# A two-layer decoder step on one core: a sixth set of expert weights, parameters as rows, inputs two pieces ahead

## What is computed

```python
def decoder_layer(x, pos, past_ckv, past_krope, h_pool, h_conv, h_sconv, mix_params, moe_params, ln_params):
    mix, st = token_mixer(x, pos, past_ckv, past_krope, h_pool, h_conv, h_sconv, *mix_params)
    x = layer_norm(ALPHA * x + mix, ln1_g, ln1_b)
    x = layer_norm(ALPHA * x + hier_moe(x, *moe_params), ln2_g, ln2_b)
    return x, st

# token_mixer: proj = x @ w_in; four branches (pooling, conformer convolution, latent
# attention, short convolution), each gated by a sigmoid; merged @ w_o
# hier_moe, 16 experts, the best 2 of one group of 4 for each token:
    h = silu(einsum('btd,edf->btef', x, w_gate)) * einsum('btd,edf->btef', x, w_up)
    h = h * comb[..., None]
    return einsum('btef,efd->btd', h, w_down)
```

## Time and profile before

| | us |
|---|---|
| median of 3 runs (lowest, highest) | 2022.55 (2022.48, 2024.47) |
| the profiled execution | 2009.65 |
| its span, first to last instruction | 2007.9 |

### The profile page before, as it was taken

One profiled execution on the slowest core, in us unless ns is written; L12 is line 12 of the kernel. 1 busy time (PEld: TensorE's weight loads), 2 busy tenths in 40 slices (PEclk: granted clock), 3 DMA queues, 4 the chain that ended last, 5 costly groups with the idle time before them and its releaser, 6 DMA issues. The chain is left out here.

```text
span 2007.9 us, 23969 instructions
## 1 busy us (share of the span) xinstructions
PE 1777.3 (89%) x9370; PEld 1205.9 (60%) x9370; DVE 799.0 (40%) x1603; ACT 445.8 (22%) x955; POOL 373.9 (19%) x398
## 2 busy tenths in 40 slices
PE   4998989999999997989569998889999999878990
PEld 3887666788888463333258776658888865533330
DVE  1596445433333350111426764554333315311116
ACT  0115534211111111111221254431111112111111
POOL 0003136000000001236100130530000004122545
PEclk6999899899999989989779988999999999889995
DMA  9203127222222647888470130443222344688984
GB/s 299 19 1 109 59 66 224 91 84 83 81 71 92 254 176 279 342 336 341 170 164 1 50 101 18 138 153 116 84 84 81 109 146 170 241 352 314 343 338 155
DMA packets 168728, 317.95 MB, mean 158 GB/s; under 512 B 63370, under 2 KB 125416, under 8 KB 150120
## 3 DMA queue, kind: packets, MB, share of 16 engines
q1 hardware_dynamic: 101144, 195.47, 27.6%
q0 software_dynamic: 37200, 116.84, 16.7%
q10 hardware_dynamic: 30272, 4.09, 1.5%
HBM read 355.74 MB, written 29.48 MB: 192 GB/s over the span
## 5 line engine op out<-in xcount | busy, mean ns | idle before, releaser
L1702 PE MATMUL ps<-space,xT 128*64 128x512 f32 x832 | 241.3, 620 | 29.5 <-DMA space<-in_exp_w_up 15.8
L1228 PE MATMUL ps<-space 128*128 128x272 f32 x1024 | 250.3, 392 | 0.0
L431 PE MATMUL ps<-xT,space 128*128 128x272 f32 (+1 forms) x960 | 225.3, 398 | 0.0
L1228 PEld LDWEIGHTS ps<-space 128*128 128x128 f32 x1024 | 194.6, 190 | 40.1
L431 PEld LDWEIGHTS ps<-xT,space 128*128 128x128 f32 (+1 forms) x960 | 184.0, 192 | 40.9
L1702 PEld LDWEIGHTS ps<-space,xT 128*64 128x64 f32 x832 | 73.5, 143 | 143.3 <-issue 140.1
L1236 PE MATMUL ps<-space 128*128 128x272 f32 x640 | 157.1, 392 | 0.0
L1959 DVE SCALAR_TENSOR_TENSOR space<-space,ps 128x256 f32<-128x256 f32 x32 | 21.5, 672 | 320.5 <-ACT space L1800 320.5
L1236 PEld LDWEIGHTS ps<-space 128*128 128x128 f32 x640 | 121.6, 190 | 25.1
L1228 PE MATMUL ps<-xT,space 128*128 128x272 f32 x512 | 128.5, 394 | 0.0
L1615 PE MATMUL ps<-space 128*128 128x512 f32 x256 | 115.7, 613 | 6.1 <-PEq L247 6.1
(11 more groups left out here) (376 smaller groups left out, 2428.5 us busy)
## 6 DMA issues: line engine op xcount, KB each, us to landing
space<-in_w_in SPq DMA_DIRECT2D x44, 1024.0 KB, 5.6
space<-in_exp_w_down SPq DMA_DIRECT2D x32, 1024.0 KB, 12.0
space<-in_exp_w_gate SPq DMA_DIRECT2D x24, 1024.0 KB, 13.1
space<-in_exp_w_up SPq DMA_DIRECT2D x24, 1024.0 KB, 14.9
space<-in_w_o SPq DMA_DIRECT2D x8, 1024.0 KB, 5.9
fifth<-in_exp_w_gate SPq DMA_DIRECT2D x8, 1024.0 KB, 17.1
fifth<-in_exp_w_up SPq DMA_DIRECT2D x8, 1024.0 KB, 19.3
space<-y_rows SPq DMA_DIRECT2D x16, 512.0 KB, 7.3
```

What stands on the lines that cost most here:

```text
L431: t = nc.tensor.matmul(ps[0:m, 2 * (n % 4) + h, 0:HN], w[:, f, c * P:c * P + m], k.xT[:, f, h, :], start=(f == 0), stop=(f == KD - 1))
L1228: t = m.matmul(out, w[:, f, :], x[:, f, :], start=(first and f == 0), stop=(f == H - 1), skip_group_check=True)
L1702: i = m.matmul(ps[r, 6 + t % 2, :], k.xgT[:, t % 2, f, r], gate_up_of(g)[:, f], start=(f == 0), stop=(f == KD - 1), skip_group_check=True)
```

## The change

It makes these edits.

1. The experts get a **sixth set** of weights, `k.sixth`, in place of the residual rows `k.x1` and of the end of `merged`. Its first load waits until the normed rows have landed in `x1_rows`; after its last use SP loads `x1` again from `x1_rows`, and DVE waits for that. All of ROUND, the loads and their semaphores follow. Tile 13 changes place with tile 9 in ORDER.
2. **Parameters are loaded as rows**: 14 DMAs put them into `prow` (43 rows) and `crow` (34 rows), PE transposes both at the head of `project` (three transposes), and ACT copies them to `k.par`. PE now waits for `s_prm`, ahead of all its work in the block. The DMAs are issued ahead of the constants by ACT in `load_start`, and by SP ahead of `first_inputs` in layer 0's `experts`. The copies into `x_rows` move from ACT in `load_start` to SP in `project`.
3. `first_inputs` issues only **two pieces** of `w_in`; the other five stand at the head of SP's queue in `project`.
4. The **landing of the stores** to `x_rows` is awaited by POOL at the head of layer 1's `project`.
5. Of the last two token tiles in layer 0, ACT turns features 0 to 3 and DVE features 4 to 7.

```diff
@@ load_start, ACT @@
             act.dma_start(k.ident[:], k.d["c_ident"]).then_inc(k.z_out, 16)
+            first_rows(k, act, 0)
...
-            for at, n, r in ROWS_OF:
-                act.dma_start(k.x_rows[at:at + r], k.d["x_prompt"][0, n:n + r, :]).then_inc(k.s_rows, 16)
...
+EARLY = 2
+def first_rows(k, queue, l):
+    d, one = k.d, bass.ds(l, 1)
+    for name, at, n in ROWS:
+        queue.dma_start(k.prow[at:at + n, :], d[name][one].rearrange("a (c p) -> (a c) p", p=P)).then_inc(k.s_prm, 16)
+    for at, lo, n, out in ((40, 0, P, 0), (41, P, QL - P, 0), (41, 0, 2 * P - QL, QL - P)):
+        queue.dma_start(k.prow[at:at + 1, out:out + n], d["q_norm_g"][one, lo:lo + n]).then_inc(k.s_prm, 16)
+    queue.dma_start(k.crow[0:CONVK, :], d["conv_w"][one].rearrange("a k n -> (a k) n")).then_inc(k.s_prm, 16)
+    queue.dma_start(k.crow[CONVK:CONVK + SCK, :], d["sconv_w"][one].rearrange("a k n -> (a k) n")).then_inc(k.s_prm, 16)
@@ first_inputs @@
-    for pos in range(SLOTS):
+    for pos in range(EARLY):
         projection(k, sp, l, pos)
@@ project: SP, ACT, POOL, PE @@
+            for pos in range(EARLY, SLOTS):
+                projection(k, sp, l, pos)
...
+            if l == 0:
+                for at, n, r in ROWS_OF:
+                    sp.dma_start(k.x_rows[at:at + r], d["x_prompt"][0, n:n + r, :]).then_inc(k.s_rows, 16)
...
-            (the 15 parameter DMAs on ACT's queue)
+            nc.scalar.copy(k.par[:, 0:43 + 2 * TAPS], ps[:, 0, 272:315 + 2 * TAPS])
...
+            if l:
+                pool.wait_ge(*due(k, n2.st, 16 * 5))
             pool.memset(k.up_p[:, :, 0:POOLH], 0.0).then_inc(k.a_zero, 1)
...
+            pe.wait_ge(*due(k, k.s_prm, 16 * 14))
+            nc.tensor.transpose(ps[:, 0, 272:315], k.prow[0:43, :], k.ident[0:43, 0:43])
+            for c in range(2):
+                nc.tensor.transpose(ps[:, 0, 315 + c * TAPS:315 + (c + 1) * TAPS], k.crow[0:TAPS, c * P:(c + 1) * P], k.ident[0:TAPS, 0:TAPS])
@@ experts @@
-ROUND = (2, 3, 0, 1, 4)
-ORDER = (0, 1, 2, 3, 4, 15, 5, 6, 14, 7, 8, 13, 9, 10, 11, 12)
+ROUND = (2, 3, 0, 1, 4, 5)
+ORDER = (0, 1, 2, 3, 4, 15, 5, 6, 14, 7, 8, 9, 13, 10, 11, 12)
...
             down(4)
+            sp.wait_ge(*due(k, n1.st, 16 * 5))
+            gate_up(5)
+            down(5)
...
+            sp.wait_ge(*due(k, k.m_dn, max(place(g) for g in USES if set_of(g) == WSETS + 1) + 1))
+            for i, (c, r) in enumerate(TOKENS):
+                sp.dma_start(k.x1[0:r, i, :], k.x1_rows[c:c + r]).then_inc(k.m_res, 16)
...
             if not last:
+                first_rows(k, sp, l + 1)
                 first_inputs(k, sp, l + 1)
...
-                pool.wait_ge(*due(k, n2.st, 16 * 5))
...
+            dve.wait_ge(*due(k, k.m_res, 16 * 10))
...
+            def turned(i, first):
+                c, r = TOKENS[i]
+                dve.wait_ge(*due(k, n2.t, i + 1))
+                for f in range(first, KD):
+                    t = v.tensor_scalar(flat[:, f, c:c + r], ps[:, 4 + 2 * (i % 2) + f // 4, (f % 4) * P:(f % 4) * P + r],
+                                        k.prm[:, f:f + 1], k.prm[:, KD + f:KD + f + 1], ALU.mult, ALU.add)
+            if not last:
+                turned(3, KD // 2)
+                turned(4, KD // 2)
```

More of the change, by code:

```diff
@@ L331, in _ @@
             sp.dma_start(d["new_conv_sample"][one, :, 0:CONVH - DS], d["state_conv"][one, :, DS:CONVH]).then_inc(k.s_kept, 16)
+            if l == 0:
+                for at, n, r in ROWS_OF:
+                    sp.dma_start(k.x_rows[at:at + r], d["x_prompt"][0, n:n + r, :]).then_inc(k.s_rows, 16)
+                for h in range(2):
+                    sp.dma_start(k.x_rows[h * HN + HP:(h + 1) * HN],
+                                 d["x_sample"][4 * h:4 * h + 4].rearrange("b t d -> (b t) d")).then_inc(k.s_rows, 16)
             projection(k, sp, l, SLOTS)
@@ L1803, in _, with turned @@
             keep_out(M - 1)
-            def turned(i):
+            def turned(i, half=KD):
                 c, r = TOKENS[i]
                 act.wait_ge(*due(k, n2.t, i + 1))
-                for f in range(KD):
+                for f in range(half):
                     t = s.activation(flat[:, f, c:c + r], ps[:, 4 + 2 * (i % 2) + f // 4, (f % 4) * P:(f % 4) * P + r], ACT.Identity,
@@ L2146, in build @@
         k.x1 = take(5, D)
+        at = queries + 4 * 2 * HN + 2 * FF + 2 * 2 * P + 2 * FF + 2 * D
+        k.sixth = take(WSET)
         k.lg = take(5, 20)
@@ L2218, in build @@
         k.m_ht, k.m_htc, k.m_dn, k.m_yA, k.m_yD = layer("m_ht", TILES), layer("m_htc", TILES), layer("m_dn", TILES), layer("m_yA", TILES), layer("m_yD", TILES)
-        loads = [sum(set_of(e) == i for e in range(NE)) for i in range(WSETS + 1)]
-        k.w_gu = [layer(f"w_gu{i}", 32 * loads[i]) for i in range(WSETS)] + [k.s_x[4]]
-        k.w_dn = [layer(f"w_dn{i}", 16 * loads[i]) for i in range(WSETS)] + [k.s_x[1]]
-        k.per_layer += [(k.w_gu[WSETS], 32 * loads[WSETS]), (k.w_dn[WSETS], 16 * loads[WSETS])]
+        loads = [sum(set_of(e) == i for e in range(NE)) for i in range(WSETS + 2)]
+        k.w_gu = [layer(f"w_gu{i}", 32 * loads[i]) for i in range(WSETS)] + [k.s_x[4], k.s_x[0]]
+        k.w_dn = [layer(f"w_dn{i}", 16 * loads[i]) for i in range(WSETS)] + [k.s_x[1], k.s_xc]
+        for i in (WSETS, WSETS + 1):
+            k.per_layer += [(k.w_gu[i], 32 * loads[i]), (k.w_dn[i], 16 * loads[i])]
         k.w_in = [layer(f"w_in{i}", n) for i, n in enumerate((112, 96, 96, 96, 112, 96, 112))]
```

51 lines of the change are left out of this document (22 added, 29 removed).

## The result

Four executions of the kernel after have a median of 1992.35 us (1991.01 to 1995.09), four of before 2023.51 (2022.48 to 2030.78). The ratio is 0.9832, 95% interval 0.981 to 0.9853: 34 us less by the ratio, between 30 and 38; the two medians differ by 31. I had forecast 49.8 us less and 1972.8; the direction was right, the size was two thirds of it. The median lies at the upper end of the range (1992), 0.35 us beyond it; by the ratio, 2022.55 would have become 1988.6.

What follows compares the result with a forecast made beforehand. PE, busy 1777 of 2008 us, was taken as the bound, so gains come from its idle time or slow clock. -22.8 - 7.0 - 22.0 + 2.0 = -49.8 us, from 2022.55 to 1972.8; range 1956 to 1992, about 0.82.

Steps and rivals of the forecast that it cites:

- start, to the first unit: Layer 0's load_start: with fewer w_in pieces issued ahead, PE's first unit begins at 16.5 instead of 39.28, 22.8 us gained.
- seam, last down to first unit: Between the layers: barrier 8.0 us earlier by POOL's earlier, shorter DRAIN, less 1.0 for transposes: 7.0 gained; layer 0's reload 0.5 lost.
- tiles, both layers: Expert tiles: a sixth weight set shortens gate and up's waits and slow clock, 11 us gained for each layer, 22 together.
- reload, layer 1: End of layer 1: reloading x1 shares the engines with the last scatter, 1.5 us lost (0 to 4).
- Less is freed: Rival: the DRAIN keeps 7.4 us, PE starts at 21.6, tiles give 6 each: -32, 1991; chance 0.2.
- The parameters: Start: last row load issued at 8.1, landing 5.5 us later at 13.6; the other end is 18.6.
- Piece 0: Start: first piece of w_in lands at 15.4, behind 4.9 MB at 0.40 to 0.42 MB/us, plus 1.5 for completion.
- Tile 3's stall: Layer 0 tiles: weights land at 789.2, due 790.6, so the 7.66 us stall is gone.
- The next two stalls: Layer 0, tiles 4 and 6: gate and up still wait 5.0 and 4.2 us for weights.
- the third: Layer 0, tile 7: stall of 4.0 us while POOL loads overflow weights on half the bandwidth, plus 1.8 of clock.
- The tiles give all: Rival: expert stalls fall under 2 us without clock cost, 27 a layer: -82, a half way -62, 1961; chance 0.13.
- Carried over: Whole kernel: the 12.9 us by which the runs' median exceeds the profiled execution before is kept in the forecast.

Runs made afterwards that it cites:

- pair order: Kernel after, but SP issues gate and up of both experts of a tile before waiting for the downs: 1949.49 us, ratio 0.9608, second measurement 0.9613.
- the kernel with columns and late pieces: Kernel after with parameters loaded as before, 15 element-wise loads on ACT's queue, no row loads or their transposes: 2013.86 us, ratio 0.9923.

## Why the prediction was right or wrong

| step | predicted | in two profiles each of before and after |
|---|---|---|
| start, to the first unit | -22.8 | 39.3, 39.5 to 18.6, 18.6: -20.8 |
| seam, last down to first unit (with layer 0's reload) | -6.5 | 49.8, 49.9 to 46.2, 46.2: -3.6 |
| tiles, both layers | -22 | 437.2, 434.7 to 423.9, 420.3: -13.9 |
| reload, layer 1 | +1.5 | 4.3, 4.3 to 7.9, 7.8: +3.6 |
| projection of layer 0 behind its first unit | 0 | 116.1, 114.7 to 116.4, 116.5: +1.0 |
| sum | -49.8 | -33.7 |

The start, the tiles and the reload came by the mechanisms that I gave, with less gained or more lost than I had put down; the seam had a wrong step. The forecast itself, 1972.8, missed by 16 to 20 us. The range only held the result, at its edge, because I had stretched it to the rival *Less is freed*. By its own steps:

*The start* was right in mechanism; both of its landings were a little late. The parameters landed at 15.1 (13.6 predicted), 9.2 us after the last issue, which began at 5.93 and not at 8.1, between the two rows that I had taken as ends. Piece 0 landed at 18.6 (15.4 predicted), and this term was mis-sized, mostly by its rate. I took 0.40 to 0.42 MB/us from the expert stage; over the first 19 us the kernel after shows 347, 286, 321 and 377 GB/s, 335 in the mean, and 4.9 MB at that rate are 14.6 us instead of 12. By 18.6 us 5.6 MB had moved, 0.7 more than I had counted, since constants and piece 1 were in flight too. The 1.5 us for completion had no row behind them; 5.6 MB at 0.335 from 1.9 on give 18.6 without them.

```profile
2.00:6.00 4.00, 1.17 (x6) 1.20 (x7) 0.04 (x1) 0.00 (x0) 1.73 (x14) 1.00 0.90 347
6.00:10.00 4.00, 4.00 (x20) 3.78 (x18) 3.35 (x5) 0.00 (x0) 0.00 (x0) 1.00 1.06 286
10.00:14.00 4.00, 2.38 (x25) 2.07 (x24) 2.50 (x6) 0.69 (x1) 0.90 (x5) 0.97 1.10 321
14.00:19.00 5.00, 3.14 (x12) 2.10 (x13) 0.00 (x0) 1.66 (x5) 0.43 (x1) 0.50 1.07 377
```

The parameters' 9.2 us are nearer to the 10.5 that I gave as the far end than to the 4.6 of the load of rot. By that row the rule of the Trainium skill ("DMA: Bandwidth & Descriptors", section "Queues, rings and completion order") that a load counts as landed only behind the earlier writes of its DMA engines may bear on this edit more than I allowed. No run here tells it from plain sharing of the engines: the load of rot, too, took 7.4 us in the kernel after. It cost little, since piece 0 came later still.

*The seam* failed in one step: "2 to 5 us" for POOL's DRAIN. I read the end of a DRAIN against what landed shortly before it, and took a coincidence (1.5 and 1.7 us) for a cause. It was my own condition for being wrong ("if POOL's drain has a length of its own"): 6.995 to 9.47 us for this block in all kernels, three times 7.403 to the nanosecond, and in seven more 7.42 from the end of the last store's issue. The 9.47 of the kernel with seven pieces (8.93 counted so) stays unexplained. What was gained is the wait for the stores: from the last store to the barrier 12.95 us became 8.1. Of these 4.8 us, 3.0 came because a store lands sooner without pieces of w_in beside it (10.0 with the wait put back), the rest because the wait is gone. The reload took back 0.5, and the longer head of the projection with its three transposes another 0.5 (1.0 predicted).

*The tiles.* Tile 3's stall went as predicted. The next two stalls were 4.4 and 4.35 (5.0 and 4.2 predicted). The term that was mis-sized is the third: 7.48 instead of 4.0, with 2.7 us of clock instead of 1.8. With the other two stalls and their clock, 16.2 + 6.9 us are left where I had 18.6 together, so the gain is 7 and not 11.6. I had let SP's loads have half of the engines beside POOL's overflow weights; from 848.0 to the landing at 868.4 POOL's queue (q0) moved more than SP's (q1): queue, packets, MB, share of the engines.

```profile
q0 software_dynamic: 645, 4.36, 53.7%
q1 hardware_dynamic: 481, 3.55, 43.1%
```

And behind the size there is a mechanism that I had in hand and did not use. I wrote that down(e) blocks the gate and up of the next, and walked the queue with it, but took that order as given and each stall as a matter of megabytes. The sixth set, 7 us a layer, only moves the blocked loads by a tile; the pair order gives 16 to 20 us more a layer. My argument against the rival *The tiles give all*, that "some stall must stay" because 6.3 MB take 15 us, was wrong too: with the queue in order no stall stays, since two of the first ten places are empty tiles that load nothing: the weights of ten experts, 31 MB or 75 us at 0.42, have the some 100 us from the first tile to the tenth. That is an argument; what is shown is the stretch with 415 GB/s and PE busy throughout.

*The Trainium skill's limit* of about 358 GB/s for one core ("DMA: Bandwidth & Descriptors", section "Specifications"), half of what the page gives a stack that two cores share, is passed again in these runs, with one core at work: 415 GB/s over 50 us in the pair kernel.

*The reload* was mis-sized: the last scatter lands in 6.2 us instead of 2.6, so it stands behind most of the 3.2 MB that I had let it share the engines with.

*Carried over*: the 12.9 us between the profile of before and its runs. That was right, and the second profile shows what they were: attend and attend_sample, 25 us shorter there in four blocks than in the second profile (merge took 4 back). Had I set my sum on the profile alone, I would have read 14.6 us of gain from the two traces and called most of the change lost.

*Rivals.* "Less is freed" (-32, 1991) is what happened, for two of its three reasons: the DRAIN kept its 7.4 us and the tiles gave 7 a layer. I had given it 0.2 because no row lets its three parts happen for one reason; they didn't need one. Three separate optimistic terms are enough. PE's new wait was 2.73 us and cost little.

## What to carry to other kernels

When a queue issues loads in a fixed order with waits between them, write down for each load when its place comes free and when the queue reaches it: a gap between the two (21.6 us here) is time for nothing, and sorting the queue costs no memory. Look for that before adding a buffer; here, against five sets in the old order, a sixth set gave 7 us a layer, the right order alone 25 to 27. And a part that lies last at a barrier can often be moved rather than shortened: let the engine with the long DRAIN finish early and give its last small job to another queue.

## What the runs showed of the hardware

- POOL's DRAIN at the end of layer 0's experts took 7.0 to 9.5 us in all fourteen profiles, with or without stores of POOL before it, and 8.2 us where POOL's part ended 34 to 36 us before the barrier. Counted from where POOL's last issue or wait ended, it is 7.40 to 7.42 us in the ten profiles with POOL's stores and two pieces ahead (or with the wait), 6.995 to 7.01 in the three without these stores, and 8.93 in the one with seven pieces beside it. It was 2.0 us in attend and 4.0 to 5.7 in attend_sample. In layer 1's experts, which end with vector work on POOL, it took 3.4 us, of which 0.12 lie behind the last vector instruction. What it is made of wasn't found.
- A load of a small parameter, an element at a time, held ACT's queue for 0.4 to 0.5 us when it was among the first, and later ones for up to 5.0 us in before and up to 8.7 us in the kernel with columns and late pieces (larger loads were still landing in both): an issue has no fixed price.
- One kernel's executions on one chip spread over 20 us (1%). A good part of it sits in attend, which took 104.5 to 116.4 us, with the mean granted clock between 0.92 and 0.82.
